# A hybrid decoder layer on one core: mix split in pieces and two output weights split inside the pair loop

## The reference

```python
z = x @ w_in + b_in                                   # 27 tiles of 128 output rows
h = mlstm_chunkwise(q, k, v, i, log_sigmoid(f), ...)  # 8 heads of 64
mix_m = sigmoid(m_o) * head_norm(h, mlstm_norm_w)     # 512 rows of mix
o_c, o_s, o_w = nsa_attend(...)                       # compressed, selected, window branches
mix_n = g0 * o_c + g1 * o_s + g2 * o_w                # 512 rows of mix
x1 = layer_norm(ALPHA * x + concat(mix_m, mix_n) @ w_out, ln1_w, ln1_b)
u = causal_dwconv(x1 @ w_up + b_up, ...)
y = layer_norm(ALPHA * x1 + (gelu(u_1) * u_2) @ w_down + b_down, ln2_w, ln2_b)
```

## Time and profile before

| | us |
|---|---|
| median of 3 runs | 911.09 |
| lowest and highest run | 909.14, 915.57 |
| the profiled execution | 908.04 |
| its span, first to last instruction | 905.9 |
| TensorE busy | 847.6 (94%) |
| VectorE busy | 591.6 (65%) |
| ScalarE busy | 409.5 (45%) |
| GpSimd busy | 136.3 (15%) |

### The profile page before, as it was taken

One profiled execution on the slowest core, in us unless ns is written; L12 is line 12 of the kernel. 1 busy time (PEld: TensorE's weight loads), 2 busy tenths in 40 slices (PEclk: granted clock), 3 DMA queues, 4 the chain that ended last, 5 costly groups with the idle time before them and its releaser, 6 DMA issues.

```text
span 905.9 us, 20084 instructions
## 1 busy us (share of the span) xinstructions
PE 847.6 (94%) x7843; PEld 769.7 (85%) x7843; DVE 591.6 (65%) x1217; ACT 409.5 (45%) x778; POOL 136.3 (15%) x256
## 2 busy tenths in 40 slices
PE   6999999899998888996899999999999999999994
PEld 6998888677886665565789999999999999999993
DVE  4632256541524898876977578888888888564555
ACT  5332255545615343765133465555556555221214
POOL 2012224342362000000100011111111111000000
PEclk9999999999997798996799999999999999999997
DMA  9268788888545000003023353222222222232222
GB/s 324 80 202 256 232 284 280 280 260 259 141 123 194 1 2 1 2 1 107 24 80 124 116 186 138 73 93 93 78 86 94 94 68 82 84 101 82 82 59 98
DMA packets 55008, 112.46 MB, mean 124 GB/s; under 512 B 7209, under 2 KB 32586, under 8 KB 54402
## 3 DMA queue, kind: packets, MB, share of 16 engines
q1 hardware_dynamic: 47074, 90.54, 30.4%
q0 software_dynamic: 6528, 17.83, 6.6%
q10 hardware_dynamic: 1312, 2.81, 1.2%
HBM read 105.54 MB, written 12.40 MB: 130 GB/s over the span
## 4 chain that ended last, share of the span: by engine, by line
PE 73%; DVE 9%; issue 6%; DMA 4%; SPq 3%; POOLq 2%; ACT 2%; POOL 0%; ACTq 0%; DVEq 0%
PE q L1909 31%; PE q L1907 28%; DMA arena<-in_pool 4%; PE q L2246 2%; DVE xt L1452 2%; PE q L2230 2%; POOLq L522 1%; PE q L1971 1%; PE q L2256 1%; SPq L522 1%; DVE xt L1465 1%; PE q L2320 1%; PE q L1959 1%; SPq L593 1%; PE q L1982 1%
## 5 line engine op out<-in xcount | busy, mean ns | idle before, releaser
L1907 PE MATMUL q<-arena_r,whi_r 128*128 128x256 f32 x712 | 210.6, 296 | 12.2 <-DVE wring_r L503 8.9
L1909 PE MATMUL q<-arena_r,whi_r 128*128 128x288 f32 (+1 forms) x712 | 212.4, 298 | 0.0
L1909 PE MATMUL q<-arena_r,wring_r 128*128 128x288 f32 (+1 forms) x712 | 212.0, 298 | 0.0
L1907 PE MATMUL q<-arena_r,wring_r 128*128 128x256 f32 x712 | 201.1, 282 | 0.0
L500 ACT ACTIVATE whi_r<-wring 128x1024 fp32r<-128x1024 f32 (+1 forms) x101 | 104.3, 1034 | 212.5 <-PE q L1909 212.1
L503 DVE TENSOR_TENSOR wring_r<-wring,whi_r 128x1024 fp32r<-128x1024 f32 (+1 forms) x101 | 120.1, 1190 | 112.3 <-ACT whi_r L500 112.0
L1909 PE MATMUL q<-xt_r,whi_r 128*128 128x290 f32 (+1 forms) x552 | 164.2, 298 | 0.0
L1907 PEld LDWEIGHTS q<-arena_r,whi_r 128*128 128x128 f32 x712 | 135.7, 191 | 23.4 <-DVE wring_r L503 8.9
L1907 PE MATMUL q<-xt_r,whi_r 128*128 128x256 f32 x552 | 155.3, 281 | 0.0
L1909 PEld LDWEIGHTS q<-arena_r,whi_r 128*128 128x128 f32 x712 | 135.8, 191 | 0.1
L1907 PEld LDWEIGHTS q<-arena_r,wring_r 128*128 128x128 f32 x712 | 135.7, 191 | 0.0
(11 more groups left out here) (468 smaller groups left out, 1554.9 us busy)
## 6 DMA issues: line engine op xcount, KB each, us to landing
wring<-in_w_up SPq DMA_DIRECT2D x42, 512.0 KB, 3.3
wring<-in_w_in SPq DMA_DIRECT2D x27, 512.0 KB, 5.3
arena<-in_pool SPq DMA_DIRECT2D x64, 192.0 KB, 4.1
arena<-in_pool POOLq DMA_DIRECT2D x64, 192.0 KB, 4.5
wring<-in_w_down SPq DMA_DIRECT2D x24, 448.0 KB, 3.3
wring<-in_w_out SPq DMA_DIRECT2D x8, 512.0 KB, 7.3
out_win_s<-in_win SPq DMA_DIRECT2D x8, 508.0 KB
arena<-in_pool SPq DMA_DIRECT2D x48, 64.0 KB, 2.2
```

The costliest lines, as they stand in the source:

```text
L1907: pe.matmul(out[:, 0, 0:HALF], w, x[:, 0:HALF], start=(kk == 0 and n == 0), stop=(end and n == 2))
L1909: mm = pe.matmul(out[:, 1, 0:width - HALF], w, x[:, HALF:width], start=(kk == 0 and n == 0), stop=(end and n == 2))
```

## The change

- **Mix is split in eight pieces** (`MIX_PIECES`). Of the attention's half: columns 0 to 255, 256 to 383, and 384 to 543; of the mLSTM's half: the 512 columns of each of its four tiles, and the sample's 32 columns of all four. The first two are made inside the loop: ScalarE in rounds 20 and 28, VectorE in rounds 21 and 29. The high parts of the attention's half move to `zt`.
- **Output weights 0 and 1 are split inside the loop** into `zt`: ScalarE in rounds 22 and 24, VectorE in rounds 23 and 25, each as two operations of 512 columns. Weight 2 is split in the tail.
- **`out_products(m, ks, c)`** does the blocks ks of output tile m for one of the two column parts (c = 0: 256 columns, c = 1: 288). Tile 0, columns 0 to 255, blocks 0 to 3 stand in rounds 27 and 28; tile 1's in rounds 33 and 34. The rest stands in the tail and in `first_tiles`, which takes the place of `out_tile(0)` and `out_tile(1)`.
- **`rows` has room for four chunks**, so all four masked parts are built ahead of the loop.
- **`token_columns`** uses two sets of banks (2, 3, 6 and 4, 5, 7), and all five groups stand in round 0.
- Output tiles take turns on `q4` the other way round, the head transposes use banks 4 and 5, and the sample's inter part banks 0 and 1.

Core of the diff:

```diff
-        rows = mixt[0:104, 0:4, :].rearrange("p k c -> p (k c)")[:, 0:1024].rearrange("p (s c) -> p s c", s=2)
+        rows = mixt[0:104, 0:4, :].rearrange("p k c -> p (k c)")[:, 0:2048].rearrange("p (s c) -> p s c", s=4)
...
+        MIX_PIECES = [(1, slice(0, 4), slice(0, HALF)), (1, slice(0, 4), slice(HALF, T - 128)), (1, slice(0, 4), slice(T - 128, NT))] \
+            + [(0, slice(t, t + 1), slice(0, T)) for t in range(4)] + [(0, slice(0, 4), slice(T, NT))]
...
-            for s in range(2):
+            for s in range(4):
                 for q in range(2):
                     pool.tensor_copy(by_block(rows[64 * q:64 * q + 8, s]),
...
-            for c in range(2):
+            for c in range(4):
                 masked_rows(c)
...
-                if i >= 2:
-                    masked_rows(i)
...
+                if m == 20:
+                    act.wait_ge(ml_s, QT)
+                    act.wait_ge(np_mx, 2)
+                    mixed_high(act, 0)
+                if m in (22, 24):
+                    out_split_hi(act, (m - 22) // 2)
+                if m == 28:
+                    act.wait_ge(np_mx, 3)
+                    mixed_high(act, 1)
...
+                if m == 21:
+                    mixed_low(dve, 0)
+                if m in (23, 25):
+                    out_split_lo(dve, (m - 23) // 2)
+                if m == 29:
+                    mixed_low(dve, 1)
...
-            for n in range(4):
-                mixed_low(n)
-            for i in range(2):
-                split_lo(dve, I_OUT + i)
+            for n in range(3, 7):
+                mixed_low(dve, n)
...
-            for n in range(4, KD):
-                mixed_low(n)
+            mixed_low(dve, 7)
+            split_lo(dve, I_OUT + 2)
...
-                for b, tiles, free, at in ((2, range(Z_MV, Z_MV + 4), tok_v_ev, i),
-                                           (3, range(Z_MK, Z_MK + 4), tok_k_ev, 2 * i - 1),
-                                           (6, (Z_CK, Z_CV, Z_SV, Z_WV), tok_k_ev, 2 * i)):
-                    if i >= 1:
+                for banks, tiles, free, at in (((2, 4), range(Z_MV, Z_MV + 4), tok_v_ev, i - 1),
+                                               ((3, 5), range(Z_MK, Z_MK + 4), tok_k_ev, 2 * i - 3),
+                                               ((6, 7), (Z_CK, Z_CV, Z_SV, Z_WV), tok_k_ev, 2 * i - 2)):
+                    b = banks[i % 2]
+                    if i >= 2:
...
+            def out_products(m, ks, c):
+
+                cols = (slice(0, HALF), slice(HALF, NT))[c]
+                out = q4[(m + 1) % 2][:, c, 0:cols.stop - cols.start]
+                for k in ks:
+                    wh = out_whi[m][k // 4][:, 128 * (k % 4):128 * (k % 4) + 128]
+                    wl = wring_r[:, (I_OUT + m) % RING, 128 * k:128 * k + 128]
+                    hi, lo = mix_hi[1 - k // 4][:, k % 4, cols], mixt_lo[:, (k + 4) % KD, cols]
+                    for n, (w, x) in enumerate(((wh, hi), (wh, lo), (wl, hi))):
+                        mm = pe.matmul(out, w, x, start=(k == 0 and n == 0), stop=(k == KD - 1 and n == 2),
+                                       skip_group_check=True)
+                return mm
...
+                if m == 27:
+                    pe.wait_ge(m_lo, 1)
+                    pe.wait_ge(w_lo, I_OUT + 1)
+                if m in (27, 28):
+                    out_products(0, (2 * m - 54, 2 * m - 53), 0)
+                if m == PAIRS + 1:
+                    pe.wait_ge(np_x, PAIRS)
+                    pe.wait_ge(w_lo, I_OUT + 2)
+                if m > PAIRS:
+                    out_products(1, (2 * (m - PAIRS) - 2, 2 * (m - PAIRS) - 1), 0)
...
+            pe.wait_ge(m_lo, 3)
+            out_products(0, range(4), 1)
             pe.wait_ge(sd_dve, 1)
...
+            def first_tiles():
+
+                pe.wait_ge(m_lo, 7)
+                out_products(0, range(4, KD), 0)
+                pe.wait_ge(sd_iv, 2)
+                out_products(1, range(4, KD), 0)
+                decode_rows()
+                pe.wait_ge(m_lo, KD)
+                out_products(0, range(4, KD), 1).then_inc(w_used, 1)
+                state_update(0)
+                state_update(1)
+                pe.wait_ge(sd_end, 2)
+                out_products(1, range(4), 1)
+                state_update(2)
+                state_update(3)
+                out_products(1, (4, 5), 1)
+                first_mean(0)
+                out_products(1, (6, 7), 1).then_inc(w_used, 1)
+                state_update(4)
+                state_update(5)
```

More of the change, by code:

```diff
@@ L1552, in _ @@
                     gated(m - 1)
[L1553 to L1554 removed]
+                if m == 0:
+                    for n in range(QT + 1):
                         token_columns(n)
```

111 lines of the change are left out of this document (63 added, 48 removed).

## The result

The changed kernel takes 915.17 us (median of 20 runs, 911.04 to 920.07), the kernel before 913.18 us (20 runs, 908.64 to 916.62). The ratio is 1.0033, with a 95% interval of 1.0017 to 1.005: slower by 2.0 us by the medians, by 1.6 to 4.6 us by the interval. The prediction put +2.0 us. The number was met, in part by luck: against the one trace that it was worked out from, the changed kernel's profile is 5.8 us longer, and that trace turned out not to be typical of the kernel before.

A forecast was written before the change was run, and what follows sets the result against it. From output tile 2 TensorE never stops, so the prediction priced when tile 2 begins: 3.0 - 1.3 + 3.9 + 0.7 - 4.3 = +2.0 us, 908.0 to 910.0 profiled, median 913.1; range 905 to 919.5.

The forecast's parts named there:

- The start: Start of the pair loop: VectorE waits for GpSimd's longer row building, cancelling the double banks; +3.0 us, between -2 and +5.4.
- −1.3 for GpSimd inside the loop: Pair loop: without GpSimd's two products beside them, two 8-element VectorE operations each run 0.65 us faster; -1.3 us.
- The middle: Loop's middle (300 to 405): VectorE's four split pieces and TensorE's products delay the pairs; +3.9 us, between +2.0 and +5.5.
- the slow rival: Pairs 21 to 26: VectorE's pieces open TensorE waits and the clock falls once, costing 3 us; 2 in 10.
- once a wait there reaches the 2.5 us: Deciding sign for a clock fall around pairs 21 to 26: a TensorE wait of 2.5 us, enough at 279.
- The end: Loop's end: six products at index 34 stand ahead of the last values; +0.7 us, between 0 and 0.7.
- The tail: From the loop to output tile 2: products already done let tile 2 begin sooner; -4.3 us, between -7 and -1.
- The 12 products: Tail: 12 products of 288 columns at half clock, 2.9 us, start the sample chain's next matmul 1.35 us late.
- The sum: Whole kernel: 3.0 - 1.3 + 3.9 + 0.7 - 4.3 = +2.0 us, profiled 908.0 becoming 910.0, median 913.1.
- The faster rival: First 30 us: GpSimd ends rows before about 275, clock holds, double banks pay; start -8, time 902; 1 in 10.

The follow-up runs named there:

- prep_first: The changed kernel, with GpSimd zeroing `tv` and `scp` after two row sets and before sets three and four: 907.96 us against 911.49, ratio 0.9965.
- start_back: The changed kernel with the start part of the kernel before (two chunks of rows, single banks): 915.26 us against 911.49, ratio 1.0026.
- start_only: The kernel before with the start part alone (rows for four chunks, double token banks): 913.87 us against 911.49, ratio 1.0021.
- loop_back: The changed kernel with the mix pieces, weight halves and 24 products moved from the loop back to the tail: 913.68 us, ratio 1.0023.
- keep_warm: The changed kernel with GpSimd's zeroing moved earlier and six transposes ahead of each probability wait in the first 12 pairs: 908.19 us against 912.53, ratio 0.9955.

## Why the prediction was right, and where it wasn't

**The start: +3.0, and −1.3 for GpSimd inside the loop; 1.7 together.** The mechanism came true as written: zeroing near 278, first pair at 278.07, a wait of about 4 us (4.08), the clock down before 279.3, and no gain from the double banks while GpSimd holds VectorE; prep_first shows that it is that wait. The two terms did not fare alike. The −1.3 was met: from pair 6's first row sums to pair 7's it takes 6.19 us in the trace that was read (303.44 to 309.63) and 4.87 in the change (310.12 to 314.99), and `L1482` and `L1484` take 0.17 us each there, as said. In the other two profiles of before only the second of the two operations lay beside GpSimd's product, and the same stretch took 5.52 and 5.53, so the term is worth 0.65 there. The term that was mis-sized is the +3.0. Against the trace that was read the start as a whole cost 3.7, so this term is 5.0, near its upper end of 5.4: the first profile of before had full clock from 300 on (above), and there it went from pair 5 to pair 6 in 3.61 us, where the change took 5.68 at 0.50. More important is what no term could hold: the base. Four profiles have the start of before (with start_back) and pair 18 at 88.58 to 94.65, mean 92.35; four have the start of the change (with start_only and loop_back) and pair 18 at 92.26 to 94.66, mean 93.02. With a spread of 6 us in the first four, that does not show that the start costs anything by pair 18.

**The middle: +3.9.** Met, nearly by its own steps. prep_first shows it without a fall of the clock: against pair 18, pair 28 comes 3.6 us later than in before (priced 3.4) and pair 30 4.0 us later (44.84 − 40.87, priced 3.9). All four pieces alone make 2.95 of it, the products 1.0; the sum had 2.5 and 1.4. In the changed kernel a fall near 402 adds 1.0: what the slow rival had, at a third of its price. The waits of TensorE behind the moved pieces grew to only 0.86 us, so the point "once a wait there reaches the 2.5 us" was wrong: the clock fell in 399 to 405 with waits far smaller ahead of it. In the kernel before it fell once in this stretch, too (second profile, near 372), without any moved piece; whether the pieces make the change's fall is open.

**The end: +0.7.** The head transposes begin 16.94 us behind pair 30 (426.01 − 409.07), against 16.31 before: +0.63.

**The tail: −4.3.** From the head transposes to tile 2's first product it takes 40.33 us (466.34 − 426.01) against 44.07 before: −3.7. Two steps inside it were off and nearly cancel. The 12 products did hold the sample's chain up: its matmul starts 1.1 us behind the end of its operand on VectorE (431.99, operand done at 430.88), where before it was 0.1. But that did not reach decode_rows, as TensorE's own work around it ran at a higher clock than before. VectorE's operand came 0.6 us sooner behind the first head transpose (the stretches from 426 have 0.80 and 0.63, those of before 0.50), and from the chain's matmul to the 128 it took 3.9 us instead of 4.8 (432 to 435 at 0.94, before 423 to 426 at 0.50) with VectorE's operations as long as before. So the matmul came 5.98 us behind the transposes, not 5.57 + 1.35 = 6.92, and decode_rows 24.48 behind, not 26.2. The next product stood 26.5 us behind the transposes, not 28.3. But from it to tile 2 it took 13.8 us (466.34 − 452.54), not the 11.4 of the sum, as the clock was 0.50 up to 462 where the sum had full clock for the second half.

**The sum.** Against the trace that it was worked out from, tile 2 comes at 466.34, 5.8 us later, and not at 462.6; pair 28 comes 8.1 us later, not 5. Of the 3.8 us that the sum lacks 2.0 are the start, 1.1 the middle and 0.6 the tail. The medians of 20 runs are nevertheless 2.0 apart, since that trace was a fast one of the kernel before: that the forecast's +2.0 was hit is luck in this part. Against the mean of the three traces of before, the first profile of the change is 0.2 us later at pair 18 and the second 0.7; both lose 4.6 from pair 18 to 30 (45.87 − 41.23) and get 3.1 back behind it (502.64 − 505.70). So the terms from the middle on were right within 0.8 each. The faster rival's mechanism was right under its own condition, in a smaller size: with GpSimd's rows done in time, pair 18 comes some 6 us sooner than in the change, where the rival had 11.

## What to carry to other kernels

Before a stage is costed from a trace, find out whether the stage repeats: a second profile of the unchanged kernel moved one mark by 4.5 us, more than the whole change was worth. Compare stages from a mark close ahead of the edit, since R alone moved by 5.7 us between traces. When rows are built earlier "for later use", put the small pieces that someone waits for ahead of the big ones: here that order was worth some 6 us of the changed kernel, and the pieces and products that were moved into the loop nothing that the runs could show.

## What was not expected of the hardware

- One program ran the first 90 us of its pair loop with 33, 43 and 48 us at half clock in three profiles, and took 88.6, 94.7 and 93.1 us for it.
- TensorE was shown as busy for 2.8 to 3.0 of each 3 us at 0.50 for more than 20 us (294 to 321 in the changed kernel), while with 12 more transposes of 128 by 128 in each of the first 12 pairs the clock stayed at 1.00 up to pair 18 (keep_warm).
- Full clock for that whole stretch was worth only 1.3 to 1.8 us, net of the transposes that bought it. In 284 to 355 of that profile VectorE was busy for 59.27 of 71 us, TensorE for 64.42; what the clock alone is worth there is not shown.
